# Hybrid attention and gated-linear-attention layer: branch merges in two token halves, with the output projection and the second norm woven into the merges and the FFN

## The chip, the cores and the metric

The kernel runs on the 8 cores of one Trainium2 chip. Each core computes 2 of the 16 batch elements, one after the other, and the cores do not talk to each other. The metric is the device time of the slowest core in microseconds (us), smaller is better. Matrix products run on TensorE (PE in the profile, with PEld for its weight loads), elementwise work on VectorE (DVE) and ScalarE (ACT), and transfers are issued by GpSimd (POOL) and SyncE (SP).

## The reference, cut to what matters

Shapes per batch element: T = 2048 tokens, D = 1024 channels, D_FF = 2816.

```python
hx = modulate(rms_norm(x, norm1_g), sh1, sc1)
...                                   # attn_o: softmax attention; gla_o: gated linear attention
go = rms_norm(gla_o, gla_norm_g).reshape(B, T, GLA_V_W) * jax.nn.silu(gla_g)      # gla_g = hx @ W_gg
ya = attn_o @ w_attn_proj
yg = go @ w_gla_proj
ga, gb = jnp.split(merge_g, 2, axis=-1)                                          # merge_g = hx @ W_m
x = x + g1 * ((jax.nn.sigmoid(ga) * ya + jax.nn.sigmoid(gb) * yg) @ w_out)       # merges, then output projection
h2 = modulate(rms_norm(x, norm2_g), sh2, sc2)                                    # second norm
a, b = jnp.split(h2 @ w_ffn_in, 2, axis=-1)
x = x + g2 * ((jax.nn.silu(a) * b) @ w_ffn_out)
```

## The kernel before, in words

Activations are kept transposed, channels on the 128 partitions: `hxT` holds the normed tokens as 8 channel tiles by 2048 tokens in bf16, and later the second norm's output in its place. Tokens are worked on in chunks `c` of 512 (four of them) and in tiles `i` of 128 (sixteen). The code is a straight program: Python loops emit instructions, each engine runs its own in the order of emission, and a small scheduler (`S.op`, `S.dma`) puts a semaphore wait before an instruction whose buffers are not ready. So one waiting instruction holds back all that is behind it on its engine or queue.

For each batch element, after the attention, the program runs these stages (lines of the kernel before):

- **Gate of the linear branch** (L1336): 8 weight tiles by 4 chunks, 8 matmuls of 512 columns each, Silu on ScalarE, one DVE product.
- **Merges** (L1357 the gate, L1364 the branch): for each of 8 output tiles `f`, for each of the two branches (`half`), for each of 4 chunks, a unit: 8 matmuls for the gate, 8 for the branch, Sigmoid on ScalarE (L1369), and one or two DVE operations (L1372 in the attention half; L1377, L1378 in the other). Result: `mT`. The two weight tiles of a pair (f, half) are loaded on the POOL queue by `load_wb` into a ring of 4 buffers, with a cast from f32, and serve 4 units.
- **Output projection and second norm**: `make_x1` loads a tile of `x` (SP queue), does 2 x 8 matmuls (L1403), two DVE operations per half row (L1406 times the gate, L1408 plus `x`) and stores the new `x` to `out` on the POOL queue. `norm_stages.stage_n` makes four such tiles, then takes Square with accumulation (L484), Ln and Exp (L486, L488) on ScalarE and scales on DVE (L492); `stage_t` transposes the group of four tiles channel tile by channel tile (8 times 4 transposes of 128 columns, L505) and writes `hxT` through ScalarE (L510), which adds scale and shift. The order is: n(0), n(1), t(0), n(2), t(1), n(3), t(2), t(3).
- **FFN in** (L1446, L1453): for each half H of 1024 tokens, for 22 weight pairs j, two units of 8 + 8 matmuls, Silu (L1457), one DVE product (L1458) into `uT`. In H = 0 the eleven pieces of the output weights (`WoG`, 512 KB each as f32 read into bf16) are loaded at j = 1 to 11 on the POOL queue.
- **FFN out** (L1500): 16 times 22 matmuls per half, with the first norm of the next batch element woven in on the second half.

`weave(main, side, lead)` merges two lists of closures: after each item of `main` it emits those of `side` that are due by their costs, such that the side list is used up at the fraction `lead` of the main one. DMA instructions are all recorded at the helper line L178.

PSUM has 8 banks. The merges use `Ring(banks[0:4])` and `Ring(banks[4:8])`, the projection 0 to 3 and the transposes 4 to 7, FFN in 0, 1 and 2, 3.

Of the kernel before, what the change touches and what calls it, by code (L numbers as in the profile page):

```python
# [11 lines left out]
D = 1024  # L12
T = 2048
# [304 lines left out]
def build(dbg=(), stop_after=99, nb=NB):  # L318
# [85 lines left out]
    goo_r = Ring([(sb("goo%d" % i, [128, 2, 256], BF16), Tk("goo%d" % i)) for i in range(2)])  # L404
    st_r = Ring([(sb("gst%d" % i, [128, 6]), Tk("gst%d" % i)) for i in range(4)])
# [147 lines left out]
    for b in range(nb):  # L553
# [765 lines left out]
        mT, mT_k, off = AB.new(0, [128, KT, T], BF16, "mT", ntk=4)  # L1319
        sg_r, off = AB.ring(off, 2, [128, 512], F32, "sg")  # L1320
        ma_r, off = AB.ring(off, 5, [128, 512], F32, "ma")
        wo0, wo0_k, _ = AW.new(0, [128, KT, 512], BF16, "wo0")
        wo_hi, wo_k, off = AB.new(off, [128, KT, 512], BF16, "wo1")
        off_x = off
        S.dma("pool", wo0, wo_d[:, :, 0:512], owner=wo0_k, writes=[wo0_k])
        S.dma("pool", wo_hi, wo_d[:, :, 512:1024], owner=wo_k, writes=[wo_k])
        bG = Ring(banks[0:4]); bY = Ring(banks[4:8])
        for f in range(8):
            wg, wg_k = take("gg%d" % f, lambda: load_wb(wb_d[WB_GG + f]))
            for c in range(4):  # L1330
                pG, pG_k = bG.next()

                def mmgg(e, pG=pG, c=c, wg=wg):
                    last = None
                    for kt in range(KT):
# [7 lines left out]
                     reads=[sg_k, goT_k[f // 2], small_k], wpart=[goT_k[f // 2]])  # L1343
        for f in range(8):
            mas = []
            for half in range(2):
                wg, wg_k = take("mg%d_%d" % (f, half), lambda: load_wb(wb_d[(WB_GA if half == 0 else WB_GB) + f]))
                wy, wy_k = take("my%d_%d" % (f, half), lambda: load_wb(wap_d[f] if half == 0 else wgp_d[f]))
                src = aoT if half == 0 else goT
                for c in range(4):  # L1350
                    pG, pG_k = bG.next()
                    pY, pY_k = bY.next()

                    def mmg(e, pG=pG, c=c, wg=wg):
# [25 lines left out]
        if b == 0:  # L1380
            dump("mT", mT.rearrange("p a b -> p (a b)"), mT_k, [128, KT * T], BF16)
        if stop_after <= 4:
            break
        x1d_k = [Tk("x1d%d" % i) for i in range(16)]
        x1_r, offA = AA.ring(0, 8, [128, D], F32, "x1t")
        xn_r, offA = AA.ring(offA, 8, [128, D], BF16, "xn5")
        xl_r, off = AB.ring(off_x, 2, [128, D], F32, "xl")
        xl2, offA = AA.ring(offA, 2, [128, D], F32, "xl2")
        xl_r = Ring(xl_r.items + xl2.items)
        st5_r, off = AB.ring(off, 3, [128, 12], F32, "st5")  # L1390
        bY5 = Ring(banks[0:4])

        def make_x1(i, ap, tk):
            xl, xl_k = xl_r.next()
            S.dma("sp", xl, x_d[b, i * 128:(i + 1) * 128, :], owner=xl_k, writes=[xl_k])
            for cc in range(2):
                ps, ps_k = bY5.next()

                def mm(e, ps=ps, cc=cc):
                    last = None  # L1400
                    for kt in range(KT):
                        rhs = wo0[:, kt, 0:512] if cc == 0 else wo_hi[:, kt, :]
                        last = e.matmul(ps, lhsT=mT[:, kt, i * 128:(i + 1) * 128], rhs=rhs, start=(kt == 0), stop=(kt == KT - 1))  # L1403
# [129 lines left out]
```

How the kernel before makes its waits and increments, by code:

```python
    def _wait(self, E, reads, writes, wpart=()):  # L117
        need = {}
        def add(sp):
            if sp is None:
                return
            k = id(sp[0])
            if k not in need or need[k][1] < sp[1]:
                need[k] = sp
        for t in reads:
            add(t.w)
            for sp in t.ws.values():
                add(sp)
            if t.excl:
                for sp in t.r.values():
                    add(sp)
        for t in writes:
            add(t.w)
            for sp in t.ws.values():
                add(sp)
            for sp in t.r.values():
                add(sp)
        for t in wpart:
            add(t.w)
            for sp in t.r.values():
                add(sp)
        for k, (sem, val) in need.items():
            if sem is E.sem and E.is_pe:
                continue
            if E.known.get(k, 0) >= val:
                continue
            E.h.wait_ge(sem, val)
            E.known[k] = val
# [40 lines left out]
    def barrier(self):  # L191
        sps = [(E.sem, E.cnt) for E in self.E.values() if E.cnt > 0]
        sps += [(o.dsem, o.dcnt) for o in self.dsems]
        for E in self.E.values():
            for sem, val in sps:
                if sem is E.sem:
                    continue
                k = id(sem)
                if E.known.get(k, 0) >= val:
                    continue
                E.h.wait_ge(sem, val)
                E.known[k] = val
```

## Time and profile before

| what | value |
|---|---|
| median of 3 runs | 3191.97 us (3191.05 to 3376.79) |
| the profiled execution | 3195.6 us, of it 3194.5 us span on core 7, the slowest |
| spans of the 8 cores | 3178.3 to 3194.5 us |
| TensorE busy | 2960.4 us, 93% of the span |
| ScalarE, VectorE, GpSimd busy | 1364.0, 1252.6, 391.1 us |
| mean granted TensorE clock, core 7 | 0.969 |
| DMA queues' share of the 16 engines | POOL's 23.0%, SP's 10.2% |

A busy share is an average over stages with different limits; the stages that the change touches are 1126 to 1366 us (batch element 0) and 2643 to 2885 us (batch element 1) of the span, and what they cost is read from windows of just these. Starts and durations of single instructions are in the timeline; an x8 behind a matmul row says that eight were merged, and the row's time is from the first one's start to the last one's end. A clock of 1.00 is the 2.4 GHz level of TensorE, and half of it the 1.2 GHz level.

### The profile page before, as it was taken

To read this page: it belongs to the slowest core of one execution; us is meant where nothing else is said; L and a number is where in the kernel's file an instruction comes from. 1 tells how busy PE (TensorE), PEld (TensorE's weight loads), DVE (VectorE), ACT (ScalarE), POOL (GpSimd) and SP (SyncE) were. 2 spreads that over 40 slices of the span, in tenths; PEclk is the share of its full clock that TensorE was granted. 3 is DMA by queue.
4 is the path that set the end of the run, shared out by engine and by line. 5 is a ranking of instruction groups with operands and counts; after the bars stand their busy time and mean duration, and the time that the engine had idled before them with its cause. 6 is when DMAs were issued, how large, how long until landed. Compare 5 with 4: busy or idle time off the path is not lost.

```text
span 3194.5 us, 55060 instructions; the slowest of 8 cores (3178.3 to 3194.5 us)
## 1 busy us (share of the span) xinstructions
PE 2960.4 (93%) x19248; PEld 1592.9 (50%) x19248; DVE 1252.6 (39%) x2306; ACT 1364.0 (43%) x2420; POOL 391.1 (12%) x707
## 2 busy tenths in 40 slices
PE   5799888999999989999988888799999998999999
PEld 1455544666544444444445654466654444444444
DVE  1444664444232262122153666444423226212222
ACT  1443567888721133101234556788872113310110
POOL 0211231000000002101100224100000000210110
PEclk8799999999999999999999999999999999999999
DMA  7533220100322259635551012010022224863542
GB/s 216 178 80 106 41 61 21 25 13 6 51 37 40 47 165 158 93 93 112 80 178 27 15 28 64 18 28 15 2 51 37 40 47 165 156 94 95 91 67 93
DMA packets 106012, 234.17 MB, mean 73 GB/s; under 512 B 9658, under 2 KB 30413, under 8 KB 105485
## 3 DMA queue, kind: packets, MB, share of 16 engines
q0 software_dynamic: 62416, 131.23, 23.0%
q1 hardware_dynamic: 43326, 99.41, 10.2%
q8 instruction: 161, 2.64, 0.3%
q14 instruction: 109, 0.89, 0.1%
HBM read 290.51 MB, written 37.75 MB: 103 GB/s over the span
## 4 chain that ended last, share of the span: by engine, by line
PE 81%; ACT 7%; DVE 5%; issue 4%; SPq 1%; DMA 1%; POOL 1%; DVEq 0%; ACTq 0%; POOLq 0%
PE ps L1446 10%; PE ps L1453 10%; PE ps L1500 9%; PE ps L1364 7%; PE ps L1357 7%; PE ps L1228 7%; PE ps L1212 6%; PE ps L669 4%; PE ps L1336 3%; PE ps L698 3%; PE ps L1012 3%; ACT sb_arenaB L1219 3%; PE ps L1403 3%; PE ps L894 2%; PE ps L505 1%
## 5 line engine op out<-in xcount | busy, mean ns | idle before, releaser
L1219 ACT ACTIVATE sb_arenaB<-ps 128x1024 bf16<-128x1024 f32 x576 | 567.2, 1023 | 70.7 <-PE ps L1212 63.2
L1457 ACT ACTIVATE sb_arenaB<-ps 128x512 f32<-128x512 f32 x176 | 105.1, 597 | 647.1 <-PE ps L1446 647.1
L1228 PEld LDWEIGHTS ps<-sb_arenaB 128*128 128x128 bf16 x4608 | 300.3, 97 | 154.1 <-issue 46.3
L1228 PE MATMUL ps<-sb_arenaB 128*128 128x129 bf16 x4608 | 353.7, 219 | 16.1 <-ACT sb_arenaB L1219 13.4
L1446 PE MATMUL ps<-sb_hxT,sb_wbuf 128*128 128x512 bf16 x1408 | 335.2, 381 | 0.0
L1453 PE MATMUL ps<-sb_hxT,sb_wbuf 128*128 128x512 bf16 x1408 | 332.6, 379 | 0.3 <-DMA sb_wbuf<-wfi 0.3
L1458 DVE TENSOR_TENSOR sb_arenaA<-ps,sb_arenaB 128x512 bf16<-128x512 f32 x176 | 121.7, 692 | 500.9 <-PE ps L1453 475.1
L1500 PE MATMUL ps<-sb_arenaB,sb_arenaA 128*128 128x512 bf16 x1408 | 308.9, 381 | 0.0
L1212 PE MATMUL ps<-sb_arenaB 128*128 128x512 bf16 x1008 | 298.9, 379 | 0.5 <-ACT sb_arenaB L1219 0.2
L1364 PE MATMUL ps<-sb_arenaA,sb_wbuf 128*128 128x512 bf16 x1024 | 241.9, 379 | 0.0
L1357 PE MATMUL ps<-sb_hxT,sb_wbuf 128*128 128x512 bf16 x1024 | 241.9, 379 | 0.0
L1369 ACT ACTIVATE sb_arenaB<-ps 128x512 f32<-128x512 f32 x128 | 76.4, 597 | 357.4 <-PE ps L1357 237.4
L1446 PEld LDWEIGHTS ps<-sb_hxT,sb_wbuf 128*128 128x128 bf16 x1408 | 138.4, 98 | 167.3 <-issue 2.9
L1453 PEld LDWEIGHTS ps<-sb_hxT,sb_wbuf 128*128 128x128 bf16 x1408 | 137.7, 98 | 166.9 <-issue 1.3
L1500 PEld LDWEIGHTS ps<-sb_arenaB,sb_arenaA 128*128 128x128 bf16 x1408 | 137.6, 98 | 164.1 <-issue 2.5
L1357 PEld LDWEIGHTS ps<-sb_hxT,sb_wbuf 128*128 128x128 bf16 x1024 | 100.2, 98 | 120.8
L1364 PEld LDWEIGHTS ps<-sb_arenaA,sb_wbuf 128*128 128x128 bf16 x1024 | 100.2, 98 | 120.8
L178 POOL DMA_DIRECT2D sb_wbuf<-wfi x176 | 94.0, 534 | 489.6 <-PE ps L1446 379.5
L669 PE MATMUL ps<-sb_hxT,sb_wbuf 128*128 128x512 bf16 x512 | 135.7, 414 | 5.5 <-DVE sb_goo L817 3.9
L783 DVE SCALAR_TENSOR_TENSOR sb_arenaB<-sb_arenaB,ps 128x256 f32<-128x256 f32 x256 | 120.4, 478 | 39.3 <-PE ps L772 17.8
L178 POOL DMA_DIRECT2D sb_wbuf<-wb x72 | 38.9, 542 | 712.4 <-PE ps L1357 323.9
L698 PE MATMUL ps<-sb_wabuf,sb_hxT 128*128 128x256 bf16 x1024 | 124.3, 276 | 0.2 <-DVE sb_goo L817 0.2
(219 smaller groups left out, 3851.5 us busy)
## 6 DMA issues: line engine op xcount, KB each, us to landing
sb_wbuf<-wfi POOLq DMA_DIRECT2D x176, 256.0 KB, 4.7
out<-sb_arenaA POOLq DMA_DIRECT2D x64, 512.0 KB, 5.2
sb_wbuf<-wb POOLq DMA_DIRECT2D x72, 256.0 KB, 4.0
sb_arenaA<-x SPq DMA_DIRECT2D x32, 512.0 KB, 6.5
sb_arenaB<-x SPq DMA_DIRECT2D x32, 512.0 KB, 5.5
sb_arenaA<-out SPq DMA_DIRECT2D x32, 512.0 KB, 4.3
sb_arenaB<-wfo POOLq DMA_DIRECT2D x22, 512.0 KB, 8.3
sb_arenaA<-w_ada SPq DMA_DIRECT2D x8, 1024.0 KB, 7.1
```

What stands on the lines that cost most here:

```text
L178: E.h.dma_start(out=out, in_=in_, **kw).then_inc(owner.dsem, 16)
L669: last = e.matmul(ps[:, 0:W], lhsT=w[:, kt, :], rhs=hchunk(c, kt)[0], start=(kt == 0), stop=(kt == KT - 1))
L698: last = e.matmul(ps[:, k * 256:(k + 1) * 256], lhsT=hsrc(i0 + k0 + k, kt)[0], rhs=wv_[:, kt, :], start=(kt == 0), stop=(kt == KT - 1))
L1212: last = e.matmul(pS[:, x, :], lhsT=kT[:, g, j * 128:(j + 1) * 128], rhs=qTx[:, h4, :], start=True, stop=True)
L1219: S.op("act", lambda e: e.activation(out=PT, in_=pS, func=AF.Exp, scale=ATT_SCALE, bias=-ATT_SHIFT), reads=pS_ks, writes=[PT_k])
L1228: last = e.matmul(oAll[:, sub, 0:129], lhsT=PT[:, x, sub * 128:(sub + 1) * 128], rhs=Vt[:, j, g, 0:129], start=(j == 0 and sub % 2 == 0), ...
L1357: last = e.matmul(pG, lhsT=wg[:, kt, :], rhs=hxT[:, kt, c * 512:(c + 1) * 512], start=(kt == 0), stop=(kt == KT - 1))
L1364: last = e.matmul(pY, lhsT=wy[:, kt, :], rhs=src[:, kt, c * 512:(c + 1) * 512], start=(kt == 0), stop=(kt == KT - 1))
L1446: last = e.matmul(pA, lhsT=wa_j[:, kt, :], rhs=hxT[:, kt, c * 512:(c + 1) * 512], start=(kt == 0), stop=(kt == KT - 1))
L1453: last = e.matmul(pB, lhsT=wb_j[:, kt, :], rhs=hxT[:, kt, c * 512:(c + 1) * 512], start=(kt == 0), stop=(kt == KT - 1))
L1458: S.op("dve", lambda e, pB=pB, sa=sa, j=j, cl=cl: e.tensor_tensor(out=uT[:, j, cl * 512:(cl + 1) * 512], in0=pB, in1=sa, op=ALU.mult), rea ...
L1500: last = e.matmul(pF, lhsT=uT[:, j, tl * 128:(tl + 1) * 128], rhs=WoG[:, j, cc * 512:(cc + 1) * 512], start=(j == 0), stop=(j == NJ - 1))
```

## The change

The merges run in two halves of 1024 tokens (`merge_items(Hh)`): a unit's two weight tiles are now loaded anew in each half. The gated branch gets one key per (f, chunk), and `mT` becomes two buffers. `wo_items(Hh, ...)` is the output projection and the second norm of one half as a list of side items: 16 half-row products `wo(i, cc)`, `rs(g)` after four tiles (Ln, Exp, four DVE scalings, then the loads of later tiles), and the transposes of a group one channel tile at a time, those of the half's first group between its later products, those of the second group at the end. The first half's list is woven into the merges of the second half, with lead 0.85; the second half's into FFN in, H = 0, with lead 0.78. The `x` tile is loaded into the buffer of the sum itself and the product goes to a small `tmp`, so the count of DVE operations stays. The stores of the new `x` move from the POOL queue to the SP queue. Six tile buffers serve the first half, four the second. PSUM: in the second half's merges 3 + 3 banks for the merges and 2 for products and transposes together; in FFN in, banks 4 to 7 for the side list. The WoG pieces are spread over j = 1 to 20.

```diff
-        for f in range(8):
-            mas = []
-            for half in range(2):
...
-                for c in range(4):
+        def merge_items(Hh):
+            wts, mas, items = {}, {}, []
+
+            def unit(f, half, c):
+                if c == 2 * Hh:
+                    wts["g"] = load_wb(wb_d[(WB_GA if half == 0 else WB_GB) + f])
+                    wts["y"] = load_wb(wap_d[f] if half == 0 else wgp_d[f])
...
+            for f in range(8):
+                for half in range(2):
+                    for c in (2 * Hh, 2 * Hh + 1):
+                        items.append((lambda f=f, half=half, c=c: unit(f, half, c), 3.4))
+            return items
...
+            def ld(i):
+                if i < 8 * Hh + 8:
+                    ap, tks = bx[i] = x1_r.next()
+                    S.dma("sp", ap, v2(x_d[b, i * 128:(i + 1) * 128, :]), owner=tks[0], writes=list(tks))
+
+            def wo(i, cc):
...
+                ps, ps_k = bank_r.next()
...
+                S.op("pe", mm, reads=[mT_k[Hh][tl // 4], wo0_k if cc == 0 else wo_k], writes=[ps_k])
+                tmp, tmp_k = tmp_r.next()
+                S.op("dve", lambda e: e.tensor_tensor(out=tmp, in0=ps, in1=G12[:, b, 0, cc * 512:(cc + 1) * 512], op=ALU.mult),
+                     reads=[ps_k, G12_k], writes=[tmp_k])
+                S.op("dve", lambda e: e.tensor_tensor(out=ap[:, cc, :], in0=ap[:, cc, :], in1=tmp, op=ALU.add),
+                     reads=[tmp_k, tks[cc]], writes=[tks[cc]])
+                if cc == 1:
+                    S.dma("sp", v2(out_d[b, i * 128:(i + 1) * 128, :]), ap, owner=tks[0], reads=list(tks), writes=[x1d_k[i]], final=True)
+                    stt, stt_k = bx["st%d" % g]
+                    S.op("act", lambda e: e.activation(out=v2(jk[0]), in_=ap, func=AF.Square, accum_out=stt[:, j:j + 1]),
+                         reads=list(tks), writes=[jk[1]], wpart=[stt_k])
+
+            def rs(g):
+                late = [i for i in range(4 * g, 4 * g + 4) if i + x1_n < 8 * Hh + 8]
...
+                S.op("act", lambda e: e.activation(out=stt[:, 4:8], in_=stt[:, 0:4], func=AF.Ln, scale=1.0 / D, bias=EPS), reads=[stt_k], writes=[stt_k])
+                S.op("act", lambda e: e.activation(out=stt[:, 8:12], in_=stt[:, 4:8], func=AF.Exp, scale=-0.5), reads=[stt_k], writes=[stt_k])
+                for j in range(4):
...
+                    S.op("dve", lambda e, xn=xn, ap=ap, j=j: e.tensor_scalar(out=v2(xn), in0=ap, scalar1=stt[:, 8 + j:9 + j], scalar2=None, op0=ALU.mult),
+                         reads=list(tks) + [stt_k], writes=[xn_k])
+                for i in late:
+                    ld(i + x1_n)
...
+            for g in (2 * Hh, 2 * Hh + 1):
+                ts = [(lambda kt=kt: t_st(2 * Hh, bx["xn%d" % (2 * Hh)], [kt]), 0.4) for kt in range(KT)] if g % 2 else []
+                for j in range(4):
+                    items.append((lambda i=4 * g + j: wo(i, 0), 1.7))
+                    if g % 2 and j > 0:
+                        items += ts[3 * (j - 1):3 * j]
+                    items.append((lambda i=4 * g + j: wo(i, 1), 1.7))
+                items.append((lambda g=g: rs(g), 0.8))
+            g = 2 * Hh + 1
+            items.append((lambda: None, 1.5))
+            items += [(lambda kt=kt: t_st(g, bx["xn%d" % g], [kt]), 0.4) for kt in range(KT)]
+            return items
+
+        for f_, _ in merge_items(0):
+            f_()
+        bG = Ring(banks[0:3]); bY = Ring(banks[3:6])
...
+        weave(merge_items(1), wo_items(0, x1_ra, tmp_r, Ring(xn_a + xn_b.items), nst_r, Ring(banks[6:8]), jk_a), 0.85)
...
-        cur = n_st(0)
-        for g in range(4):
-            nxt = n_st(g + 1) if g < 3 else None
-            t_st(g, cur)
-            cur = nxt
...
+        bside = wo_items(1, x1_rb, tmp_b, xn_rb, nst_r, Ring(banks[4:8]), jk_b)
...
+        wog_at = {1: 0, 3: 1, 5: 2, 7: 3, 9: 4, 11: 5, 13: 9, 15: 10, 18: 6, 19: 7, 20: 8}
...
         for H in range(2):
...
+            if H == 0:
+                weave(ffn_in(0), bside, 0.78)
...
+            else:
+                for f_, _ in ffn_in(1):
+                    f_()
```

## Rows read from the trace of the kernel before

**Rows 1.** Windows by stage; columns: window, length, busy by engine, clock, DMA share, GB/s

```profile
core 7: us, PE busy (x) PEld busy (x) DVE busy (x) ACT busy (x) POOL busy (x), PEclk, DMA share, GB/s
904.90:1126.10 221.20, 221.20 (x1026) 100.29 (x1025) 65.97 (x96) 40.09 (x66) 15.33 (x29) 1.00 0.25 40
1126.10:1213.70 87.60, 71.53 (x386) 35.22 (x384) 56.33 (x82) 40.74 (x71) 11.55 (x21) 0.89 0.58 179
1213.70:1366.50 152.80, 152.80 (x706) 69.13 (x704) 29.73 (x43) 29.52 (x48) 30.07 (x53) 0.99 0.77 118
...
2643.00:2731.30 88.30, 72.15 (x386) 35.41 (x384) 56.34 (x82) 40.80 (x71) 11.55 (x21) 0.88 0.56 179
2731.30:2885.30 154.00, 153.67 (x705) 69.15 (x704) 29.75 (x43) 29.46 (x48) 30.07 (x53) 0.99 0.72 116
```

**Rows 2.** Timeline of TensorE in the projection stage: gaps, transposes, the last group

```profile
1162.49 2.59 PE L505 MATMUL ps<-sb_ident_bf,sb_arenaA 128*128 128x128 bf16 x16 [5.89 <-ACT sb_hxT L510]
1164.88 3.25 PE L1403 MATMUL ps<-sb_wabuf,sb_arenaB 128*128 128x512 bf16 x8
1167.96 1.89 PE L1403 MATMUL ps<-sb_arenaB 128*128 128x512 bf16 x8
...
1205.79 7.94 PE L505 MATMUL ps<-sb_ident_bf,sb_arenaA 128*128 128x128 bf16 x48 [3.42 <-ACT sb_hxT L510]
```

**Rows 3.** Chain that ended last: 256 matmuls of 512 columns without a gap; start, us

```profile
849.84 55.25 PE ps L1336 x256
```

**Rows 4.** Timeline, woven transposes in FFN out, second half of batch element 0

```profile
1668.97 0.28 PE L505 MATMUL ps<-sb_ident_bf,sb_wabuf 128*128 128x128 bf16 x2
1669.08 4.91 PE L1500 MATMUL ps<-sb_arenaB,sb_arenaA 128*128 128x512 bf16 x22
```

**Rows 5.** Windows, the untouched second FFN in and the later part of the woven FFN out

```profile
1442.40:1594.40 152.00, 152.00 (x706) 68.95 (x705) 31.12 (x45) 27.11 (x45) 23.26 (x44) 1.00 0.55 90
1626.00:1690.00 64.00, 64.00 (x389) 32.73 (x388) 33.33 (x57) 14.79 (x27) 3.42 (x6) 1.00 0.46 157
```

**Rows 6.** Timeline, end of a group of four tiles on ScalarE and VectorE

```profile
1142.03 1.06 ACT L484 ACTIVATE sb_arenaA<-sb_arenaA 128x1024 bf16<-128x1024 f32 x1 [2.60 <-DVE sb_arenaA L1408]
...
1143.25 1.28 ACT L486 ACT_TABLE_LOAD   x1
1144.55 0.20 ACT L486 ACTIVATE sb_arenaB<-sb_arenaB 128x4 f32<-128x4 f32 x1
...
1145.16 2.74 DVE L492 TENSOR_SCALAR sb_arenaA<-sb_arenaA,sb_arenaB 128x1024 bf16<-128x1024 f32 x4 [3.22 <-ACT sb_arenaB L488]
```

**Rows 7.** Groups by line in the projection stage: the two DVE forms, ScalarE's write of `hxT`

```profile
L1406 DVE TENSOR_TENSOR sb_arenaA<-ps,sb_G 128x512 f32<-128x512 f32 x32 | 22.1, 691 | 12.7 <-PE ps L1403 12.2
L510 ACT ACTIVATE sb_hxT<-ps,sb_mod2T,sb_sc2e 128x512 bf16<-128x512 bf16 x30 | 20.3, 793 | 0.0
```

**Rows 8.** Timeline of POOL's queue in FFN in: weight loads of two pairs

```profile
1234.15 0.56 POOL L178 DMA_DIRECT2D sb_wbuf<-wfi  x1 [3.94 <-PE ps L1446]
1235.88 0.53 POOL L178 DMA_DIRECT2D sb_wbuf<-wfi  x1 [1.18 <-PE ps L1453]
...
1241.06 0.56 POOL L178 DMA_DIRECT2D sb_wbuf<-wfi  x1 [3.94 <-PE ps L1446]
```

**Rows 9.** DMA issues, 905 to 1126 us (merges): count, KB each, median us to landing

```profile
sb_wbuf<-wap POOLq DMA_DIRECT2D x7, 256.0 KB, 4.6
```

**Rows 10.** DMA issues, 1126 to 1213 us (projection): count, KB each, us to landing

```profile
out<-sb_arenaA POOLq DMA_DIRECT2D x16, 512.0 KB, 6.0
...
sb_arenaA<-x SPq DMA_DIRECT2D x6, 512.0 KB, 7.0
sb_wbuf<-wfi POOLq DMA_DIRECT2D x4, 256.0 KB, 8.1
```

**Rows 11.** DMA issues, 1213 to 1366 us (FFN in): count, KB each, us to landing

```profile
sb_wbuf<-wfi POOLq DMA_DIRECT2D x43, 256.0 KB, 5.0
```

More of the change, by code:

```diff
@@ L1327, in build @@
         bG = Ring(banks[0:4]); bY = Ring(banks[4:8])
+        goH_k = []
+        for f in range(8):
+            goH_k.append([])
+            for c in range(4):
+                t_ = Tk("goH%d_%d" % (f, c))
+                inherit(t_, goT_k[f // 2])
+                goH_k[f].append(t_)
+                AA.live.append((f * 1024 + c * 256, f * 1024 + c * 256 + 256, t_))
         for f in range(8):
@@ L1380, in build @@
[L1380 to L1383, printed above, removed]
-        x1d_k = [Tk("x1d%d" % i) for i in range(16)]
[L1385 to L1390, printed above, removed]
@@ new lines, in wo_items @@
+            x1_n = len(x1_r.items)
+            for x in range(x1_n):
+                ld(8 * Hh + x)
+            for g in (2 * Hh, 2 * Hh + 1):
[6 more added lines that the diff above has]
+                items.append((lambda g=g: rs(g), 0.8))
@@ new lines, in wo_items @@
+            g = 2 * Hh + 1
[5 more added lines that the diff above has]
+        bG = Ring(banks[0:3]); bY = Ring(banks[3:6])
+        x1_ra = Ring([dead_pair(0, a) for a in range(4)] + [dead_pair(8192, a) for a in range(2)])
+        xn_a = [AA.new(8192 + 1024 * f, [128, D], BF16, "xnA%d" % f)[0:2] for f in range(4, 8)]
@@ L1423, in build @@
         uT, uT_k, offA = AA.new(0, [128, NJ, 1024], BF16, "uT", ntk=2)
-        xr6_r, offA = AA.ring(offA, 2, [128, D], F32, "xr6")
-        stg_r, offA = AA.ring(offA, 2, [128, D], F32, "stg")
-        WoG, WoG_kj, off = AB.new(0, [128, NJ, D], BF16, "WoG", ntk=11)
-        sa_r, off = AB.ring(off, 2, [128, 512], F32, "sa")
+        x1_rb, offA = AA.ring(offA, 4, [128, 2, 512], F32, "x1b", )
+        x1_rb = Ring([(ap, (tk, Tk("x1bh"))) for ap, tk in x1_rb.items])
+        for _, tks in x1_rb.items:
+            inherit(tks[1], tks[0])
@@ new lines, in build, with ffn_in, unit, mma @@
+        wog_at = {1: 0, 3: 1, 5: 2, 7: 3, 9: 4, 11: 5, 13: 9, 15: 10, 18: 6, 19: 7, 20: 8}
+        def ffn_in(H):
+            wts, items = {}, []
+            def unit(j, cl):
+                if cl == 0:
+                    wts["a"] = take("fa%d_%d" % (j, H), lambda: load_wb(wfi_d[j]))
+                    wts["b"] = take("fb%d_%d" % (j, H), lambda: load_wb(wfi_d[NJ + j]))
+                    if H == 0 and j in wog_at:
+                        load_wog(wog_at[j])
+                wa_j, wa_jk = wts["a"]
+                wb_j, wb_jk = wts["b"]
+                c = 2 * H + cl
+                pA, pA_k = bA.next()
+                pB, pB_k = bB.next()
+                def mma(e):
+                    last = None
+                    for kt in range(KT):
+                        last = e.matmul(pA, lhsT=wa_j[:, kt, :], rhs=hxT[:, kt, c * 512:(c + 1) * 512], start=(kt == 0), stop=(kt == KT - 1))
+                    return last
+                S.op("pe", mma, reads=[wa_jk, hxT_k[c]], writes=[pA_k])
+                def mmb(e):
+                    last = None
+                    for kt in range(KT):
+                        last = e.matmul(pB, lhsT=wb_j[:, kt, :], rhs=hxT[:, kt, c * 512:(c + 1) * 512], start=(kt == 0), stop=(kt == KT - 1))
+                    return last
+                S.op("pe", mmb, reads=[wb_jk, hxT_k[c]], writes=[pB_k])
+                sa, sa_k = sa_r.next()
+                S.op("act", lambda e: e.activation(out=sa, in_=pA, func=AF.Silu), reads=[pA_k], writes=[sa_k])
+                S.op("dve", lambda e: e.tensor_tensor(out=uT[:, j, cl * 512:(cl + 1) * 512], in0=pB, in1=sa, op=ALU.mult),
+                     reads=[pB_k, sa_k], wpart=[uT_k[cl]])
+            for j in range(NJ):
+                for cl in range(2):
+                    items.append((lambda j=j, cl=cl: unit(j, cl), 3.4))
+            return items
```

151 lines of the change are left out of this document (72 added, 79 removed).

## The prediction, made before the changed kernel ran

> **What bounds the kernel now.** I read the spans and clocks of the cores first, then the chain that ended last, then windows by stage. TensorE is 93% busy and ends nearly everything, so an edit is worth what it takes off TensorE's own time: idle time, time at the lower clock, matmuls that wait. The windows show where such time is. The merges are free of it: 221.2 us, all busy, clock 1.00 [rows 1]. FFN in is too, where nothing goes before it: 152.0 us [rows 5]. The output projection with the second norm is not: 87.6 us and 88.3 us, of them 71.5 and 72.2 busy, at a mean clock of 0.89 and 0.88, and FFN in behind it takes 152.8 and 154.0 us where 152.0 would do, because the clock is still low at its start [rows 1, 5]. The timeline shows why: a group's transposes wait for Square, Ln, Exp and the scaling of the group before, and TensorE stands still 5.89 us, then 3.42 us; after the first the next eight matmuls take 3.25 us instead of 1.89, that is 1.2 GHz instead of 2.4. At the end twelve groups of four transposes take 7.94 us, 0.66 each, with no other work for TensorE between them [rows 2]. Other engines are at 64% (DVE) and 47% (ACT) even there [rows 1].
>
> **The change, part by part.** First, the stage's own work stays, and is what it costs at best. 256 matmuls of 512 columns take 55.25 us when nothing stops them [rows 3]. 128 transposes: two of them take 0.11 us from start to start when woven [rows 4], so 64 x 0.11 = 7.1 us. Together 62.4 us for each batch element, 124.8 for both. What there is to gain: 87.6 + 88.3 = 175.9 us of stage, plus 0.8 + 2.0 = 2.8 us of FFN in over 152.0, minus 124.8, is 53.9 us. That is the ceiling: the matmul counts of all stages are unchanged.
>
> Second, does the weaving hide the waits? A unit of the merges takes 221.2 / 64 = 3.45 us, with 40.09 / 64 = 0.6 us of ScalarE and one or two DVE operations of 0.69 [rows 1]. In the second half 32 units (110.6 us, half of 221.2) carry 16 products and 64 transposes (31.2 us): 142 us. DVE has 33 us of its own and half the stage's 56.3, ACT 20 and half of 40.7 [rows 1], so 43% and 28%: no engine becomes the bound. In FFN in it is 152 + 31 = 183 us with DVE 30 + 28, less still. The later part of FFN out is the proof that this form of weaving works: transposes, DVE and ScalarE steps of a norm between matmuls, and 64.00 us busy of 64 [rows 5].
>
> What is left are places where TensorE catches up with the queues. By the costs in the code a side list is 36.7 long and a unit makes 1.35 of it due in the merges (3.4 x 36.7 / 92.5) and 1.07 in FFN in (3.4 x 36.7 / 116.7). Working the weave out, products come every 1.26 and 1.59 units, and the transposes of the first half fall behind units 14 (one, after a product), 15 (two), 18 (three), 21 (two, after a product), 25 (three), 26 (four) and 27. They share two banks with the products. A third in a row waits until ScalarE has read the first: 0.1 + 0.79 + 0.07 us [rows 7] after it, less the 0.22 of the second: about 0.75 us; a fourth 0.45 more (0.66 a group when ScalarE sets the pace [rows 2], minus 0.22). So 0.75 behind units 18 and 25, 1.2 behind 26. Behind 21 the third user waits for DVE's product (0.69 us [rows 7]): 0.65. Sum 3.35 us for each batch element. In FFN in the side list has four banks, and never more than three transposes in a row: nothing.
>
> **rs(g).** From the last product: two DVE steps (1.6 us with their gaps [rows 7]), then from Square's start to the last of four scalings 1145.16 + 2.74 - 1142.03 = 5.9 us [rows 6], 7.5 in all. Queued behind them are Sigmoid or Silu and the DVE product of the next units, and for the banks of these units TensorE comes back after three units (3 banks) or two (2 banks): 10.4 and 6.9 us, the latter plus a product. After g = 0 and g = 2 the next user of the result is at least four units away, nothing waits. After g = 1 and g = 3 the first transpose is due two units later, at 6.9 us: 0.6 to 0.7 us late. Two such places: 1.4 us. The switch between the tables of Ln/Exp and of Sigmoid or Silu now comes twice per rs, 16 in all instead of once per stage; it takes 1.28 us on ScalarE [rows 6], hidden by ScalarE's idle time, and one of them is in the 7.5 us.
>
> The Trainium skill (ScalarE: Activation LUTs, What ACT_TABLE_LOAD costs) adds a drain of 1.38 us to a load of 1.28, which speaks against this change. This trace agrees with the load but shows no drain: from the load's start to the next ACTIVATE it is 1.30 us [rows 6]. By the skill's figure the four late transposes would be 1.4 us later each, 5.5 us in all; the trace decides.
>
> So stalls of 3.35 + 1.4 = 4.75 us for each batch element, 9.5 for both. Bounds, as the trace has no such place: none at all below; above, every group of transposes at ScalarE's pace (32 x 0.44 = 14.1 us) and a gap of 3.42 us [rows 2] at each of four rs (13.7), 55.6 us for both elements, which would eat the whole gain. I take 9.5, near the lower end, because rows 5 is the nearest case and has none.
>
> **Weights.** The merges load each pair twice, 64 instead of 32 tiles per element. A pair then serves 6.9 us, exactly FFN in's rhythm [rows 8]. A buffer is freed when its last matmul ends and needed again 6.9 + 1.7 = 8.6 us later; loads land after 4.6 us in the merges, 5.0 in FFN in with the WoG pieces in the same queue [rows 9, 11]: cost nothing. DMA share: 0.25 x 221.2 = 55 us of engine time for 32 tiles [rows 1], so 0.50 in the first half; in the second 55 + 25 (half of 0.58 x 87.6) in 142 us, 0.56; in FFN in (117.7 + 25) / 183 = 0.78 beside 0.77 before. Stores of the sum move from POOL's queue to SP's, behind which only loads of `x` wait. Those of the second half are the risk: tiles 12 to 15 are loaded only when 8 to 11 are scaled, land 7.0 us later [rows 10], and hold DVE at the sum for perhaps 1.5 us; TensorE's banks allow about 4. Nothing. The six first loads go out at once at the half's start (7.0 us) and the first sum is due at 9. WoG pieces end at j = 20 with 20 us left.
>
> **The sum.** 53.9 - 9.5 = 44.4 us. The profiled execution took 3195.6 us (span 3194.5 and 1.1 around it): 3151 for such a one. The median of the runs shown is 3.6 us below it, so 3148.
>
> **The rivals.**
> - *The queues hold TensorE more often than worked out.* ScalarE and DVE are in order, and each rs holds up Sigmoids and products behind it. For it: rows 2's gaps are of just this chain. Against: rows 5. At half the upper bound the stalls are 28 us, the gain 26: 3166 (3157 to 3192). Chance 0.18.
> - *Slower: the doubled weight loads come late.* Place: all merge pairs and FFN in's first half. For it: a load landed after 8.1 us where `x` and `out` moved [rows 10], 0.5 us below the 8.6 allowed. It decides at 44.4 us / (2 x (32 + 22) = 108 pairs) = 0.41 us a pair, that is at a landing of 9.0 us all along; at 10 us it costs 108 x 1.4 = 151 us: 3299. Against: 5.0 us with the queue at its fullest [rows 11], and the woven pairs leave more room. Chance 0.08, half of it beyond 2%.
> - *The clock.* The gaps were the only rest between 850 and 1594 us. Were TensorE granted 1.2 GHz for a tenth of the new unbroken 740 us in each element, 148 us would be lost: 3296. Against: 221.2 us at 1.00 [rows 1] and 152.0 behind a full FFN stage at 1.00 [rows 5]. Chance 0.04. The Trainium skill (TensorE: Matmul & The Clock Gate, Part 1) says that a die is held at 13/16 of the clock once three cores run dense matmuls; here all eight do so in these stages and the granted clock is 1.00, so the trace does not agree.
> - *More than the ceiling*, by something in a stage that I took as untouched: 3130. Chance 0.06.
> - *Forecast*: stalls of 0 to 18 us, 3138 to 3157. Chance 0.64.
>
> **From these the numbers.** The range 3134 to 3180 takes all of the forecast, most of the first rival and most of the last: 0.64 + 0.13 + 0.04 = 0.81. 2% of 3192 is 64 us, about what a measurement of this kernel tells from no change. Faster than 3128 needs more than the ceiling: 0.02. Slower than 3256: half the weights' chance and half the clock's, 0.06. Within: 0.92.
>
> **What would show it.** In the changed profile: the second merges half about 142 us and FFN in about 183 + 1 us with PE busy all through, clock 1.00 from 850 to 1594 us less the gain; gaps of TensorE under 1.3 us at transposes, put down to L510's counterpart, two of some 0.7 us per element at the first transposes after rs; no wait of a matmul for a weight load; landing of weights below 8 us. Wrong would be: a wait on weight loads, a gap over 3 us behind an rs, TensorE's clock below 1.00 in the merges, or DVE waiting for `x` so long that a matmul waits for a bank.

## The result, and the profile after

The changed kernel takes 3152.17 us (median of 12 runs), the kernel before 3192.26 us in 12 runs on the same chips: a ratio of 0.9876, 95% interval 0.9853 to 0.9898. That is 40 us, inside the range of 3134 to 3180, 4 us above the forecast of 3148, and within 2% as forecast. Three of the 12 runs of the changed kernel and one of the kernel before had one die at a lower granted clock and were 6 to 13% longer; without such runs the medians are 3150.54 and 3191.97 us (41.4 apart), and the ratio above and all times and comparisons below leave them out.

The page of the profiled execution (3153.3 us, span 3152.0 on core 1), cut to the busy times and the two queues that carry the loads:

```profile
PE 2941.8 (93%) x19248; PEld 1585.7 (50%) x19248; DVE 1249.7 (40%) x2306; ACT 1382.7 (44%) x2434; POOL 407.6 (13%) x739
...
q0 software_dynamic: 67024, 131.23, 25.3%
q1 hardware_dynamic: 52030, 116.19, 11.5%
```

Between the two profiled cores (core 7 before, core 1 after) TensorE's busy time fell by 19 us: the transposes that ran at ScalarE's pace and the matmuls at 1.2 GHz are shorter now. 5.5 us of it lie in the attention of element 1 (602.4 and 596.9 us busy), which the change does not contain; the account of the prediction comes back to that. The rest of the gain is idle time. q0 carries the merges' weights twice.

The stretch that the change touches is from the first matmul of the gate to the first of FFN out. The chain that ended last gives it for each core by the starts of two merged rows; core 7, the counterpart of [rows 3] (start, us, what):

```profile
834.99 55.25 PE ps L1347 x256
1332.04 75.97 PE ps L1590 x352
...
2328.96 55.25 PE ps L1347 x256
2825.72 75.97 PE ps L1590 x352
```

1332.04 - 834.99 = 497.05 us, and 496.76 in element 1. The same difference before is 516.7 to 518.7 us on the eight cores, 517.9 in the mean of both elements. By the prediction's terms (the gate, the merges, the stage's own work, FFN in) it takes 55.25 + 221.2 + 62.4 + 152.0 = 490.9 at best.

The windows by stage, core 7, the counterpart of [rows 1] (window, length, busy by engine, clock, DMA share, GB/s): gate, first merges half, second merges half with the first half's projection and norm, FFN in H = 0 with the second half's, FFN in H = 1.

```profile
core 7: us, PE busy (x) PEld busy (x) DVE busy (x) ACT busy (x) POOL busy (x), PEclk, DMA share, GB/s
834.90:890.20 55.30, 55.30 (x259) 25.07 (x257) 23.65 (x32) 19.73 (x32) 3.74 (x7) 1.00 0.22 34
890.20:1000.80 110.60, 110.60 (x514) 50.10 (x512) 32.59 (x47) 21.02 (x34) 16.91 (x32) 1.00 0.52 74
1000.80:1148.00 147.20, 142.71 (x706) 66.25 (x705) 60.39 (x88) 45.33 (x72) 17.02 (x32) 1.00 0.57 121
1148.00:1332.00 184.00, 183.19 (x897) 84.87 (x896) 58.49 (x85) 53.59 (x85) 31.40 (x55) 1.00 0.73 141
```

The stages of 87.6 and 88.3 us are gone; their work lies in the third and fourth row, at clock 1.00 throughout on this core. What is lost is 147.20 - 142.71 = 4.5 us idle in the second merges half and 0.8 us in FFN in.

TensorE's waits in these stages on core 1, the slowest (total us, times, longest; both elements):

```profile
PE ps L506 <- ACT sb_hxT L511: 6.1, 9, 1.1
...
PE ps L1532 <- DMA sb_wbuf<-wfi: 3.3, 2, 2.6
...
PE ps L506 <- DVE sb_arenaB L1456: 3.2, 4, 0.8
...
PE ps L506 <- DVE sb_arenaB L1437: 1.4, 2, 0.7
```

Three of the four are the waits of transposes that were forecast. 0.5 of the 6.1 us belongs to the first norm, so they are (5.6 + 3.2 + 1.4) / 2 = 5.1 us for each element in rounded totals; summing the gaps one by one gives 5.28 in element 0 and 5.0 in element 1, where the first of them is 0.80 instead of 1.08. The fourth, a matmul of FFN in that waits for its weights, was said not to happen.

The timeline of TensorE on core 1 shows the forecast ones in place (start, us, engine, line, operation, count, idle before and its releaser):

```profile
1103.02 0.61 PE L506 MATMUL ps<-sb_ident_bf,sb_arenaA 128*128 128x128 bf16 x8
1104.71 0.38 PE L506 MATMUL ps<-sb_ident_bf,sb_arenaA 128*128 128x128 bf16 x4 [1.08 <-ACT sb_hxT L511]
1104.93 1.89 PE L1372 MATMUL ps<-sb_hxT,sb_wbuf 128*128 128x512 bf16 x8
...
1119.85 0.38 PE L506 MATMUL ps<-sb_ident_bf,sb_arenaA 128*128 128x128 bf16 x4 [0.72 <-DVE sb_arenaB L1437]
...
1136.58 0.61 PE L506 MATMUL ps<-sb_ident_bf,sb_arenaB 128*128 128x128 bf16 x8 [0.80 <-DVE sb_arenaB L1456]
1137.98 0.38 PE L506 MATMUL ps<-sb_ident_bf,sb_arenaB 128*128 128x128 bf16 x4 [0.80 <-ACT sb_hxT L511]
...
1143.11 0.38 PE L506 MATMUL ps<-sb_ident_bf,sb_arenaB 128*128 128x128 bf16 x4 [0.80 <-ACT sb_hxT L511]
1143.78 0.38 PE L506 MATMUL ps<-sb_ident_bf,sb_arenaB 128*128 128x128 bf16 x4 [0.28 <-ACT sb_hxT L511]
```

A third transpose group in a row waits for ScalarE to free one of two banks; at 1136.58 the first group after `rs(1)` waits for the scaling. A seventh, 0.80 us, lies at 1306.84 after `rs(3)`. And after a gap of 1.08 us the next eight matmuls still take 1.89 us, that is 2.4 GHz, unlike those after 5.89 us in [rows 2].

The one that was not forecast, all engines of core 1 at the start of FFN in:

```profile
1153.56 0.53 POOL L178 DMA_DIRECT2D sb_wbuf<-wfi  x1 [4.88 <-PE ps L1372]
...
1154.99 1.80 SPq L178 DMA_DIRECT2D sb_arenaA<-x  x4
1155.29 0.53 POOL L178 DMA_DIRECT2D sb_wbuf<-wfi  x1 [1.20 <-PE ps L1379]
...
1161.49 1.89 PE L1525 MATMUL ps<-sb_hxT,sb_wbuf 128*128 128x512 bf16 x8
...
1166.00 3.18 PE L1532 MATMUL ps<-sb_hxT,sb_wbuf 128*128 128x512 bf16 x8 [2.62 <-DMA sb_wbuf<-wfi]
...
1168.97 2.33 PE L1525 MATMUL ps<-sb_hxT,sb_wbuf 128*128 128x512 bf16 x8
```

The four `x` tiles of the second half, 2 MB, go out together on SP's queue at 1154.99. The second weight tile of FFN in's first pair goes out at 1155.29 and is there at 1166.0, 10.7 us later, where [rows 11] had 5.0. TensorE stands 2.62 us, and the next eight matmuls take 3.18 us instead of 1.89, the eight after them 2.33. Together 2.8 + 1.3 + 0.4 = 4.5 us, and the stretch of this core is 1350.23 - 848.69 = 501.54 us, 4.5 more than core 7's. Windows of core 1 over the same time:

```profile
1155.00:1160.00 5.00, 5.00 (x25) 2.28 (x24) 2.00 (x3) 0.60 (x1) 0.53 (x1) 1.00 0.93 220
1160.00:1165.00 5.00, 3.38 (x16) 1.35 (x14) 1.39 (x2) 2.13 (x3) 1.77 (x3) 1.00 1.01 270
1165.00:1170.00 5.00, 4.00 (x11) 1.53 (x12) 0.00 (x0) 0.35 (x1) 0.00 (x0) 0.66 1.07 202
```

The DMA engines are full (share 0.93 to 1.07) for 15 us, and the granted clock is 0.66 after the gap. Six of the eight cores have such a wait, of 0.7 to 2.6 us, in one or both elements (five of them in element 0). The fall of the clock does not follow from the length of the gap alone: cores 1, 3 and 5 have it in element 0 after 2.62, 2.27 and 2.29 us, but on core 3 in element 1, after a gap as long as core 1's, the matmuls go on at 2.4 GHz:

```profile
2651.14 1.89 PE L1532 MATMUL ps<-sb_hxT,sb_wbuf 128*128 128x512 bf16 x8 [2.60 <-DMA sb_wbuf<-wfi]
```

### The profile page after: what moved, and what is told of

The parts are those of the page before. It is cut to its first block, busy times and chain, and to the rows that moved or that the text cites. A ratio compares the mean times of both kernels' runs of the same rounds, so it can differ in the third digit from the quotient of the medians.

```text
span 3152.0 us, 54975 instructions; the slowest of 8 cores (3130.6 to 3152.0 us)
## 1 busy us (share of the span) xinstructions
PE 2941.8 (93%) x19248; PEld 1585.7 (50%) x19248; DVE 1249.7 (40%) x2306; ACT 1382.7 (44%) x2434; POOL 407.6 (13%) x739
## 3 DMA queue, kind: packets, MB, share of 16 engines
q8 instruction: 160, 2.62, 0.3%
## 4 chain that ended last, share of the span: by engine, by line
PE 81%; ACT 7%; DVE 4%; issue 4%; DMA 2%; SPq 1%; POOL 1%; DVEq 0%; ACTq 0%; POOLq 0%
PE ps L1590 10%; PE ps L1532 9%; PE ps L1525 9%; PE ps L1229 7%; PE ps L1372 7%; PE ps L1379 7%; PE ps L1213 6%; PE ps L699 4%; PE ps L1433 4%; PE ps L1347 4%; PE ps L670 3%; PE ps L1013 3%; ACT sb_arenaB L1220 3%; PE ps L895 2%; SPq L178 1%
## 5 line engine op out<-in xcount | busy, mean ns | idle before, releaser
L1532 PE MATMUL ps<-sb_hxT,sb_wbuf 128*128 128x512 bf16 x1408 | 333.9, 380 | 3.3 <-DMA sb_wbuf<-wfi 3.3
L1532 PEld LDWEIGHTS ps<-sb_hxT,sb_wbuf 128*128 128x128 bf16 x1408 | 137.8, 98 | 170.5 <-issue 5.3
L178 POOL DMA_DIRECT2D sb_wbuf<-wb x104 | 56.1, 540 | 831.5 <-PE ps L1372 346.9
```

What stands on the lines that cost most here:

```text
L178: E.h.dma_start(out=out, in_=in_, **kw).then_inc(owner.dsem, 16)
L1532: last = e.matmul(pB, lhsT=wb_j[:, kt, :], rhs=hxT[:, kt, c * 512:(c + 1) * 512], start=(kt == 0), stop=(kt == KT - 1))
```

## The experiments

Theory A: the gain is idle and slow time of TensorE that the weaving fills; what is left of it are (i) waits of transposes for two shared banks, (ii) waits at the scaling after `rs(1)` and `rs(3)`, (iii) the weight load held up by four `x` tiles. Rival B: part of the gain comes from the split itself, or the split's double weight loads and the table switches on ScalarE cost something that hides elsewhere. The measure is the stretch from gate to FFN out beside the whole time, because the time of the slowest core scatters by several us for reasons that lie ahead of the change: a core's gate starts at 835 to 852 us of the span. Over the 96 cores of the twelve profiles this start goes with the waits for the `w_ada` loads at the beginning (16 to 28 us in total, correlation 0.66) and, more closely, with the time at 1.2 GHz ahead of it (55 to 92 us, correlation 0.83). Core 1 of the changed kernel is the slowest by the second of these: it has 92 us, the other cores 58 to 79.

**Split without weaving (e1).** Both side lists run after the merges, one behind the other; loads, halves, banks and buffers are those of the changed kernel.

```diff
-        weave(merge_items(1), wo_items(0, ...), 0.85)
+        aside = wo_items(0, ...)
+        for f_, _ in merge_items(1) + aside:
+            f_()
...
-                weave(ffn_in(0), bside, 0.78)
+                for f_, _ in bside + ffn_in(0):
+                    f_()
```

> Both side lists run behind one another instead of woven: the first half's after the second half's merges, the second half's ahead of FFN in. Halved merges, doubled weight loads, stores on SP's queue and the bank counts stay. My theory: the gain is the weaving alone, so it is all given back and a little more, since each half now has its own exposed end (rs to the last group's transposes 7.5 us, eight transposes at 0.66 us) and the first half has only two banks: 88 to 105 us of stage for each element against 62 + 6 now, so 3192 to 3225 us. Rival (halves as such give the gain, or the old order of stores and loads was the fault): it stays near 3152 to 3165 us. Rival (doubled weight loads cost something that the weaving hid): TensorE would wait on weight loads in the merges; my theory says none.

Measured: 3225.09 us, 1.0102 times the kernel before (1.0086 to 1.0118), 75 us above the changed kernel's 3150.54. Windows of core 4: gate and all merges, both projections, FFN in.

```profile
848.20:1124.70 276.50, 276.25 (x1281) 124.94 (x1279) 89.40 (x127) 59.79 (x98) 37.71 (x71) 1.00 0.48 79
1124.70:1230.10 105.40, 76.95 (x389) 36.74 (x388) 56.17 (x82) 42.56 (x72) 1.25 (x2) 0.83 0.44 150
1230.10:1382.00 151.90, 151.90 (x703) 68.80 (x702) 29.73 (x43) 28.54 (x47) 30.15 (x53) 1.00 0.67 108
```

The merges with doubled loads take 276.5 us, what gate and merges took before (55.25 + 221.2): the doubled loads cost nothing there (at most 1.5 us of waits on some cores). The projection stage is worse than the 87.6 us of [rows 1], since a half ends with nothing beside its scaling and transposes: 105.4 us, of them 28.5 idle, at clock 0.83. The stretch is 533.8 and 534.3 us on core 4, so the split without the weaving, its two banks and moved stores included, loses 16 us per element, and the weaving wins 74.6 / 2 = 37 us by the times, 35 by the stretches. Rival B's gain from the split is out.

**One side serial at a time (e8, e9).** e8 takes the weave out of the merges only, e9 out of FFN in only (the first or the second hunk above).

> Only the first half's projection and norm run unwoven, behind the second half's merges; the second half's stay woven into FFN in. With both unwoven it took 73 us more than with both woven. Theory (each half hides about as much, the first a little more since its unwoven form has two banks only): 38 to 45 us more than the changed kernel, 3190 to 3197 us. Rival (one of the weaves does nearly all): 3160 or 3220 us.

> The counterpart of e8: the second half's projection and norm run unwoven ahead of FFN in, the first half's stay woven. Both unwoven cost 73 us, the first alone about 41 (3193.9 against 3152 to 3156), with 517 to 518 us from the gate stage to FFN out instead of 497. Theory (the two weaves are independent): the rest, 31 to 35 us, 3184 to 3189 us, the stretch 514 to 516 us. Rival (one unwoven stage moves its stalls onto the other): less than 25 or more than 40.

Measured, one execution each: 3193.93 us (e8) and 3184.17 us (e9), 43.4 and 33.6 above the changed kernel, 77.0 together where e1 has 74.6. By the stretches (means of eight cores, both elements) it is 38.5 + 34.8 = 73.3 where e1 has 70.7. So the two weaves help or hinder each other by no more than some 3 us, and one execution each can't tell that from nothing. TensorE's wait at the scaling, in e8, for both elements:

```profile
PE ps L506 <- DVE sb_arenaB L1456: 15.3, 4, 6.9
```

Its longest is 6.9 us; woven, it is 0.8.

**The `x` loads one by one (e2).** One tile of the second half is loaded at the start, the next each when a product begins.

```diff
+                if cc == 0 and Hh and 8 <= i < 11:
+                    ld(i + 1)
...
-            for x in range(x1_n):
+            early = 1 if Hh else x1_n
+            for x in range(early):
```

> Of the second half's first four x tiles only the first is loaded ahead; each of the other three with the product of the tile before it. In the changed kernel TensorE waited 1.0 to 2.6 us at the first FFN unit of element 0 for a weight load on six of eight cores, and ran its next matmuls at 1.2 GHz. Theory (the four x tiles, 2 MB issued at once within 0.3 us of that weight load, delay it): the wait is gone on all cores, the stretch from the gate stage to FFN out takes 497 us on all cores in element 0 instead of 501 to 502, the slowest core gains 3 to 5 us: 3148. Rival (the WoG piece or the rhythm of the weight loads at the stage's change): the wait stays.

Measured: 3151.01 us, ratio 0.9865 (0.9843 to 0.9886). The wait for weights on core 1 is down from 2.62 to 0.13 us (L1535 is L1532 of the changed kernel):

```profile
1159.86 1.89 PE L1528 MATMUL ps<-sb_hxT,sb_wbuf 128*128 128x512 bf16 x8
...
1161.88 1.89 PE L1535 MATMUL ps<-sb_hxT,sb_wbuf 128*128 128x512 bf16 x8
```

The stretch is 497.1 to 497.4 us on all eight cores in element 0, where it was up to 501.5, and 496.7 to 497.7 in element 1, with 0.3 to 0.8 us of wait left on three cores. This supports cause (iii). The whole time did not move: the slowest core of the profiled execution started its gate at 852.44 us, after 27.6 us of waiting for `w_ada` where the others had 18 to 22. The mean span of the eight cores is 3139.7 against 3140.6. So the gain is seen in the stretch (1.8 us in element 0 and 0.8 in element 1, means of eight cores) and too small for the whole time to show. How late the weights come also differs between executions of the changed kernel: in e6 the wait is at most 2.0 us, no core's clock falls in the stretch, and e2 is better than it by 1.0 us over both elements.

**Four banks for the side list (e3).** The merges of the second half take 2 + 2 banks instead of 3 + 3.

```diff
-        bG = Ring(banks[0:3]); bY = Ring(banks[3:6])
+        bG = Ring(banks[0:2]); bY = Ring(banks[2:4])
...
-        weave(..., Ring(banks[6:8]), jk_a), 0.85)
+        weave(..., Ring(banks[4:8]), jk_a), 0.85)
```

> In the second half's merges the banks are split 2 + 2 + 4 instead of 3 + 3 + 2, as in FFN in. Theory (transposes wait because they share two banks): the waits of transposes for ScalarE and for the product on DVE go (6.1 and 1.4 us in the page of the changed kernel, nearly all in the merges), only the two waits of 0.8 us for the scalings stay for each element; two banks for each side of the merges are enough, since TensorE comes back after 6.9 us and more; 5 to 7 us less, 3146. Rival (the merges need the third bank behind an rs): new waits of the merges' matmuls for Sigmoid or DVE, 1 to 3 us at each rs, 3152 or more.

Measured: 3142.21 us, ratio 0.9839 (0.9823 to 0.9855). Core 2, both elements:

```profile
PE ps L506 <- DVE sb_arenaB L1456: 3.2, 4, 0.8
...
PE ps L506 <- ACT sb_hxT L511: 0.5, 1, 0.5
```

Cause (i) is gone in full: 6.1 us went to 0.5 (the first norm's), the wait for DVE's product at L1437 no longer appears, the waits at the scaling stay, and the merges do with 2 + 2 banks. The stretch is 492.5 to 494.2 us, with up to 1.5 us of the wait for weights.

**Spread transposes (e4).** Banks as in the changed kernel. The costs of the first half's transposes are raised so that fewer fall due together, the empty item that keeps distance from `rs` is doubled in both halves, and the first half's list ends with the merges.

```diff
-                ts = [(... t_st(2 * Hh, ...), 0.4) for kt in range(KT)] if g % 2 else []
+                ts = [(... t_st(2 * Hh, ...), 0.4 if Hh else 1.0) for kt in range(KT)] if g % 2 else []
...
-            items.append((lambda: None, 1.5))
-            items += [(... t_st(g, ...), 0.4) for kt in range(KT)]
+            items.append((lambda: None, 3.0))
+            items += [(... t_st(g, ...), 0.4 if Hh else 1.0) for kt in range(KT)]
...
-        weave(merge_items(1), wo_items(0, ...), 0.85)
+        weave(merge_items(1), wo_items(0, ...), 1.0)
```

> Costs in the weave changed only: transposes of the first half cost 1.0 instead of 0.4 and its lead is 1.0, so at most two fall behind a unit; the empty item ahead of the last eight is 3.0 instead of 1.5 in both halves, so that three units stand between rs and the first transpose. Theory: waits behind three and four in a row go, and so do the 0.8 us waits for the scalings in both halves; 4.5 to 5.5 us for each element, 3142 to 3144. Rival (any transpose that is woven costs a wait, wherever it is put): the waits of transposes stay at about 10 us over both elements.

Measured: 3139.07 us, ratio 0.9826 (0.9809 to 0.9844). Windows of core 4 (first merges half, second, FFN in):

```profile
890.20:1000.80 110.60, 110.60 (x515) 50.14 (x513) 32.57 (x47) 20.98 (x34) 16.91 (x32) 1.00 0.52 75
1000.80:1141.60 140.80, 140.80 (x696) 65.52 (x695) 60.27 (x88) 43.90 (x70) 16.91 (x32) 1.00 0.58 128
1141.60:1325.60 184.00, 184.00 (x907) 85.52 (x906) 58.35 (x85) 54.81 (x87) 31.31 (x56) 1.00 0.75 140
```

No idle time at all: 435.4 of 435.4 us busy at clock 1.00, and the stretch is 490.63 us, the bare sum of its matmuls. Causes (i) and (ii) are gone, by the order of emission alone. A few waits for weights of 0.4 to 1.8 us stay on three cores, as e4 leaves the four `x` loads.

**Both (e5, e10), and the changed kernel again (e6).** The diffs of e2 and e4 together; e6 is the changed kernel beside e5.

> The two edits of e2 and e4 together. The stretch from the gate stage to FFN out was 490.6 us in e4 where no weight load was late, which is the sum of its matmuls (55.25 + 221.2 + 62.4 + 151.9 = 490.8 us). Theory (the two waits are separate): 490.6 us on every core and in both elements, TensorE waits for no weight load in FFN in, 3136 to 3139 us, 13 to 16 below the changed kernel beside it. Rival (spreading moves the last transposes up to FFN in and with them new collisions of transfers): late weight loads remain on some cores and it equals e4.

> The changed kernel itself beside its variants: 3152 us, 0.987 to 0.988 of the kernel before.

> e5 once more for a narrower interval: ratio to the kernel before 0.982 to 0.984, 3135 to 3142 us, that is 10 to 14 us below the changed kernel's 3152.

Measured: e5 3138.02 us with a ratio of 0.9806 (0.9728 to 0.9885; the runs of the kernel before beside it scattered, so it tells little), e6 3154.51 us, ratio 0.9859 (0.9800 to 0.9917), with waits at the same places as the first profile; those for the two banks and the scaling have the same lengths, those for weights are shorter (0.1 to 2.0 us). e10, the same kernel as e5: 3135.28, 3135.84 and 3135.92 us, ratio 0.9819 (0.9800 to 0.9839) to a kernel before of 3191 to 3195 us. Its stretch is 490.6 to 491.8 us on the eight cores, with one wait for weights of 0.7 us left. This version beats both kernels: 3135.8 us, 15 below the changed one. That it beats e4 is not shown: their ratios overlap, and over both elements the stretches differ by 0.3 us.

**Weights loaded anew for each chunk (e7).** A test of how far the rival with the late weights was away: each unit loads its own pair, twice the loads of the changed kernel.

```diff
-                if c == 2 * Hh:
+                if True:
```

> In both halves of the merges the two weight tiles are loaded for every unit, 128 tiles for each element instead of 64: the doubling of the loads once more. 32 tiles took 0.25 x 221.2 us of the DMA engines, 1.73 us each, so two in a unit of 3.45 us fill them, and a load has 5.2 us from a free buffer to its use. Theory (loads had 8.6 us and landed after 4 to 5, so the first doubling cost nothing, the second brings them to the edge): waits for weight loads in the merges, 10 to 60 us in all, 3160 to 3215. Rival (loads are far from binding): 3152, no such wait.

Measured, one execution: 3212.51 us, 62 above the changed kernel. Windows of core 2, its slowest, in the first and in the woven second merges half:

```profile
905.00:1010.00 105.00, 93.16 (x410) 38.83 (x417) 27.32 (x40) 15.52 (x26) 27.80 (x53) 1.00 0.88 131
1010.00:1150.00 140.00, 130.27 (x605) 58.40 (x615) 52.66 (x78) 33.73 (x55) 30.14 (x57) 0.99 0.88 164
```

TensorE's waits for weights on the same core (total us, times, longest):

```profile
PE ps L1372 <- DMA sb_wbuf<-wb: 21.7, 31, 1.9
...
PE ps L1379 <- DMA sb_wbuf<-wgp: 13.3, 13, 3.7
PE ps L1379 <- DMA sb_wbuf<-wap: 11.2, 11, 2.7
```

A pair now serves 3.45 us and each load still lands in 5.1 to 5.4 us (median); with four buffers TensorE waits 46 us in 55 places. The rival's mechanism exists, and the changed kernel is one doubling away from it.

## Why the prediction was right, and where not

- **The ceiling, 53.9 us: right.** The stretch fell from 517.7 and 518.2 us (elements 0 and 1, means of eight cores) to a floor, seen in e4 and e10, of 490.63 and 490.91: 54.3 us for both.
- **Weaving hides the waits of Square, Ln, Exp and scaling: right.** Gaps of 5.89 and 3.42 us [rows 2] became 0.80. ACT and DVE are at 31% and 41% in the woven merges (45.33 and 60.39 of 147.2) where 28% and 43% were worked out; the DMA shares are 0.52, 0.57 and 0.73 for 0.50, 0.56 and 0.78.
- **The remaining stalls, 4.75 us per element: right in place, a little small in size.** Behind units 18, 21, 25 and 26: 1.08, 0.72, 0.80 and 0.80 + 0.28 for 0.75, 0.65, 0.75 and 1.2; after `rs(1)` and `rs(3)` 0.80 each for 0.6 to 0.7. The sum is 5.28 in element 0 and 5.0 in element 1. (Of the first term's 0.1 + 0.79 + 0.07 only ScalarE's 0.79 had a row.) What was missing is that a gap costs more than the idle time shown: 497.05 - 490.63 = 6.4 us for seven gaps, 0.16 more for each, and 496.75 - 490.91 = 5.8 in element 1, 0.12 more for each. The timeline of core 1 shows why: a group with work behind it takes 0.22 us (from 1104.71 to 1104.93), so two take 0.44, but before a gap they take 0.61 (the 1103.02 row), since the last one's end is not overlapped by a next matmul, and from there 1.08 us are idle. e3 and e4 take these places away one by one.
- **The table switches: right.** 25 loads in the execution where there were 11: 14 more, which is the forecast of 16 in these stages instead of one per stage. ScalarE's idle time hides them. The rows of core 7 at `rs(0)`, to be read against [rows 6]:

```profile
1118.10 1.28 ACT L1450 ACT_TABLE_LOAD   x1
1119.39 0.21 ACT L1450 ACTIVATE sb_nst<-sb_nst 128x4 f32<-128x4 f32 x1
...
1119.91 1.28 ACT L1384 ACT_TABLE_LOAD   x1
1121.21 1.09 ACT L1384 ACTIVATE sb_arenaB<-ps 128x512 f32<-128x512 f32 x2
```

  From the load's start to the next ACTIVATE it is 1.29 and 1.30 us. The drain of 1.38 us of the Trainium skill (ScalarE: Activation LUTs, What ACT_TABLE_LOAD costs) would put the second at 1122.6; it is at 1121.21. The late transposes would have waited some 2.2 us; they waited 0.80.
- **Weights, in the merges: right.** They land in 3.8 to 4.8 us (median of `wb`, `wgp`, `wap` in the first half), and no matmul waits for them.
- **Weights, at FFN in: the step that failed.** "Cost nothing" took the landing time of the steady stage, 5.0 us, for the first pair too. The prediction looked at what tiles 12 to 15 do to DVE and not at what the loads of tiles 8 to 11, all at once, do to the two weight loads issued 1.4 us before and 0.3 us after them. [rows 10] had the warning (8.1 us beside `x` and `out`), and it was used only for a whole stage of late loads. It cost 3.0 us in the mean of eight cores over both elements (1.4 in e6), and 4.5 in element 0 of the slowest core. The size is small because it happens once per element.
- **The clock: right but for one place.** It is 1.00 in each of core 7's windows above, 497 us in which no gap is over 1.08 us. On five of the eight cores it is so in both elements; on cores 1, 3 and 5 it falls for a moment behind the late weights of element 0, as shown (0.66 in the window from 1165). In e6 it falls on no core. The 13/16 of the Trainium skill (TensorE: Matmul & The Clock Gate, Part 1) does not appear in these windows, with all eight cores at it.
- **The sum.** The ceiling of 54.3 us, less 12.3 for the seven gaps of each element, less 3.0 for the late weights, is 39.1 us from the two stretches (mean core) where 44.4 was forecast.
- **What came from outside the stretches.** 4.9 us more came from a part in which the change only moves buffers of the woven first norm: from FFN out's start in element 0 to the gate of element 1 it is 994.3 us, before 999.2 (means of eight cores). 0.5 of it is the woven part of FFN out, 4.4 is the attention behind it, 671.6 us where it was 676.0. TensorE's idle time there is nearly the same (75.8 and 76.3 us); what differs is the clock. By the trace's clock records a core has 1.2 GHz for 44 to 51 us of the attention before (mean 47.8), and for 34 to 44 us after (mean 38.4). The first 15 us of it, core 7 before and core 4 after (the clock is the third figure from the end, 0.66 and 1.00):

```profile
1689.00:1704.00 15.00, 10.55 (x59) 5.95 (x58) 4.05 (x9) 4.50 (x6) 2.12 (x4) 0.66 0.56 105
```

```profile
1654.00:1669.00 15.00, 10.73 (x88) 6.87 (x87) 4.55 (x10) 7.06 (x10) 2.12 (x4) 1.00 0.51 107
```

  All eight cores have this low stretch before, five of eight after. Over the 96 cores of the twelve profiles the length of the attention goes with this time (correlation 0.96; 0.43 us longer for each us at 1.2 GHz), so the 9.4 us less of it are worth 4.0 of the 4.4. The buffers are not the reason: e1 has the same ones, without the weaving, and has 676.2 us and 49.5 at 1.2 GHz. What sets where the low stretches fall stays open. The last 2.2 us lie ahead of the first gate (842.4 and 840.1 us in the mean), in the scatter told above. Together the mean core gained 46.2 us, the slowest 3194.5 - 3152.0 = 42.5, and the medians of the runs 40.1 to 41.4. So the forecast came within 4 us partly by luck: the unforeseen gain in the attention made up for the late loads (3.0) and for gaps of 12.3 us instead of 9.5.

Of the rivals, *the queues hold TensorE more often* fell by rows that count seven gaps, all under 1.1 us. *The weights come late* is true in one place and not along the merges, and e7 shows from where on it decides. *The clock* and *more than the ceiling* did not come about, though the 4.4 us in the attention are a small piece of the last. The clock's price of 148 us was twice too high as worked out: at half speed a tenth of the time loses half of that tenth, 74 us.

## What to carry to other kernels

When independent matmul work exists, weave a stage's chain of small steps into it and count the places that are left: who shares a bank, how many users in a row, how long after the last scaling the first reader comes. Those places can then be moved by the order of emission alone (12.3 us in the two stretches here). At each seam between stages, ask which bulk loads go out in the same microsecond as a weight load that is needed next, and read the landing time of that moment, not the stage's median.

## What the runs showed of the hardware that was not expected

- A 256 KB weight load issued 0.3 us after four loads of 512 KB on another queue landed after 10.7 us; the same load takes 5.0 us in the steady stage, and with one `x` load at a time instead of four TensorE waits 0.1 us for it on that core instead of 2.6 (e2).
- After 2.62 us of idle time TensorE's next eight matmuls took 3.18 us and the granted clock of that window was 0.66, so that this gap cost 4.5 us; after 2.60 us at the same place in element 1 of core 3 they took 1.89 us, as after all gaps of up to 1.08 us.
- A gap in a dense row of matmuls costs 0.12 to 0.16 us more than the idle time in its row (means over seven gaps).
- Cores of one execution reach the gate up to 16 us apart (835 to 851 us in e4), by the time at 1.2 GHz and the waits for the first loads; which core is last changes from run to run, and this hides changes of 2 us and less in the time of the slowest.
- One and the same attention stage took 670 to 678 us on the 96 cores, and its length goes with how long TensorE was at 1.2 GHz in it (34 to 58 us, correlation 0.96); the mean idle time in it is 75.6 to 76.3 us in every run.
